# Dense expert values: sums kept in the eight PSUM banks and added once, tiles read by one 4 MB transfer in runs of 32 KB

## The reference, cut to what matters

```python
eidx = jnp.take_along_axis(cidx, sel, axis=-1).reshape(T, PEER_HEADS * PEER_TOPK)   # 128 experts per token
gate = jax.nn.softmax(sc, axis=-1).reshape(T, PEER_HEADS * PEER_TOPK).astype(c.dtype)
def expert_block(args):
    xb, idx, g = args
    act = jax.nn.gelu(jnp.einsum('td,tkd->tk', xb, u[idx]), approximate=False)
    return jnp.einsum('tk,tkd->td', g * act, v[idx])
```

## Time and profile before

| | |
|---|---|
| time, median of 3 runs | 3749.01 us (3737.89 to 3749.76) |
| the profiled execution's own time | 3740.18 us |
| its span | 3738.4 us |
| busy PE, DVE, ACT, POOL | 83%, 74%, 17%, 36% of the span |
| DMA | 1471.37 MB, mean 394 GB/s |
| build stage | about 2100 to 2376 us of the span |
| dense stage (L1239, L2212) | 2376 to 3379 us |
| embed beside the rows of SB, then the last block | 3379 to 3687, then to 3738 us |

### The profile page before, as it was taken

How to read it: one execution, slowest core, us unless ns; L and a number is a source line. 1 busy time by engine, 2 the same in 40 slices (tenths; PEclk the granted TensorE clock), 3 DMA queues, 4 the chain that set the end, 5 groups by cost and what they waited for, 6 DMA issues and landing times.

```text
span 3738.4 us, 26646 instructions
## 1 busy us (share of the span) xinstructions
PE 3101.5 (83%) x9234; PEld 1887.3 (50%) x9234; DVE 2756.7 (74%) x3846; ACT 636.9 (17%) x1610; POOL 1352.5 (36%) x908
## 2 busy tenths in 40 slices
PE   8998697999977359999988654799989899896955
PEld 4547343544456124455436643566666666563422
DVE  1005988677677869887866897978878899877785
ACT  2211110132011122122201366200000000002102
POOL 0001543325235434333333522423434342435552
PEclk9999798999988679999998856799999999998987
DMA  8889999999999999999999998999999999999997
GB/s 276 280 275 335 419 417 418 417 418 419 417 412 405 415 375 412 417 417 417 377 393 400 388 371 329 405 422 421 421 421 414 421 421 421 400 420 416 400 411 308
DMA packets 319143, 1471.37 MB, mean 394 GB/s; under 512 B 26080, under 2 KB 64416, under 8 KB 180768
## 3 DMA queue, kind: packets, MB, share of 16 engines
q0 software_dynamic: 129840, 944.83, 61.5%
q1 hardware_dynamic: 179136, 513.18, 36.1%
q10 hardware_dynamic: 10032, 11.66, 0.9%
HBM read 1443.88 MB, written 25.69 MB: 393 GB/s over the span
## 4 chain that ended last, share of the span: by engine, by line
DMA 39%; PE 22%; DVE 12%; issue 6%; POOL 6%; ACT 3%; SPq 0%; DVEq 0%; POOLq 0%; ACTq 0%
DMA ring<-in_peer_v,eidx 17%; PE psum L926 13%; DMA ring<-in_peer_u,eidx 11%; POOL ring L862 6%; DVE ring L2327 5%; DMA W<-in_w_peer_q 5%; DMA W<-in_w_out 2%; PE psum L904 2%; DVE arena L2339 2%; PE psum L1189 2%; DMA W<-in_w_ple_gate 1%; DMA a_scratch<-arena 1%; PE psum L1315 1%; ACT arena L1653 1%; DVE W L2195 1%
## 5 line engine op out<-in xcount | busy, mean ns | idle before, releaser
L2327 DVE CUSTOM_DVE_ANT_0 ring<-ring,cx 128x2048 f32<-128x2048 f32 x576 | 1312.5, 2285 | 235.1 <-DMA ring<-in_peer_u,eidx 232.3
L862 POOL DMA_INDIRECT ring<-in_peer_u,eidx x576 | 878.3, 1525 | 1676.4 <-DVE dots L2327 1255.1
L2339 DVE SCALAR_TENSOR_TENSOR arena<-ring,wts,arena 128x2048 f32<-128x2048 f32 x320 | 751.6, 2349 | 215.5 <-DMA ring<-in_peer_v,eidx 197.7
L926 PE MATMUL psum<-W,actT 128*128 128x512 f32 x1792 | 793.0, 601 | 19.2 <-DVE arena L2045 10.4
L862 POOL DMA_INDIRECT ring<-in_peer_v,eidx x320 | 469.1, 1466 | 617.9 <-DVE arena L2339 576.7
L926 PEld LDWEIGHTS psum<-W,actT 128*128 128x128 f32 x1792 | 342.0, 193 | 437.0 <-issue 420.3
L904 PE MATMUL psum<-W,actT 128*128 128x512 f32 x832 | 375.8, 608 | 42.4 <-issue 31.0
L1189 PE MATMUL psum<-actT,W 128*128 128x128 f32 (+2 forms) x1536 | 288.5, 353 | 83.1 <-DMA W<-in_w_peer_q 72.0
L1189 PEld LDWEIGHTS psum<-actT,W 128*128 128x128 f32 x1536 | 262.9, 208 | 107.8 <-DMA W<-in_w_peer_q 78.9
L904 PEld LDWEIGHTS psum<-W,actT 128*128 128x128 f32 x832 | 161.3, 196 | 243.4 <-issue 228.5
L1787 ACT ACTIVATE gel<-dots 128x8 f32<-128x8 f32 x72 | 15.1, 209 | 1572.8 <-DVE dots L2327 1572.7
(11 more groups left out here) (318 smaller groups left out, 2319.0 us busy)
## 6 DMA issues: line engine op xcount, KB each, us to landing
W<-in_w_in SPq DMA_DIRECT2D x168, 1024.0 KB
W<-in_peer_v SPq DMA_DIRECT2D x64, 1024.0 KB
arena<-in_peer_v SPq DMA_DIRECT2D x64, 1024.0 KB
W<-in_w_out SPq DMA_DIRECT2D x48, 1024.0 KB
W<-in_w_peer_q SPq DMA_DIRECT2D x48, 1024.0 KB
W<-in_w_ple_gate SPq DMA_DIRECT2D x39, 1024.0 KB
ring<-in_peer_u,eidx POOLq DMA_INDIRECT x576
a_scratch<-W SPq DMA_DIRECT2D x8, 1024.0 KB
```

Source lines behind the costliest of these rows:

```text
L862: pool.indirect_dma_start(ring[:, slot, :], None, a["peer_u" if what == "u" else "peer_v"][0], off(ix, 0)).then_inc(ring_in[slot], 16)
L926: ins = pe.matmul(bank(4 * s + j), lhs(at_k, j), w_pair(q)[:, k, s * CG:(s + 1) * CG], start=(at_k == 0), stop=(at_k == KT - 1))
L2327: dve.tensor_tensor_reduce(row, row, cx[:, :], 1.0, 0.0, ALU.mult, ALU.add, dots[:, n % DEEP, c:c + 1]).then_inc(u_used, 1)
L2339: dve.scalar_tensor_tensor(out=hslot(t), in0=ring[:, slot, :], scalar=wts[:, n % DEEP, c:c + 1], in1=hslot(t), op0=ALU.mult, op1=ALU.add). ...
```

## The change

Each tile is now one transfer of 4.19 MB in which partition p gets experts 4p to 4p + 3 of the tile, 32 KB in a row. So A's two indices change: within a tile's 512 experts the set is the number's lowest two bits, the partition the next seven. The results of all 32 tiles are summed in PSUM, in the eight banks, and DVE adds four times in all, at positions 529.6 to 532.6. The turn of `p` needs banks 6 and 7, so its wait for the adds moves ahead of it.

```diff
@@ row_landed
-                return tiles_in[k % 2], 16 * (VT * NVG // 2 + 1)
+                return tiles_in[k % 2], 16 * (NVG // 2 + 1)
@@ load_tiles
-            for x in range(VT):
-                e0 = (m * VT + x) * NKEY
-                sp.dma_start(v_tiles(m)[:, x, :], a["peer_v"][0, e0:e0 + NKEY, :]).then_inc(tiles_in[m % 2], 16)
+            e0 = m * VT * NKEY
+            sp.dma_start(v_tiles(m), a["peer_v"][0, e0:e0 + VT * NKEY, :].rearrange("(p x) d -> p x d", x=VT)).then_inc(tiles_in[m % 2], 16)
@@ pe_dense
-                pe.wait_ge(tiles_in[m % 2], 16 * VT * (m // 2 + 1))
+                pe.wait_ge(tiles_in[m % 2], 16 * (m // 2 + 1))
                 for i in range(4):
-                    at = 4 * m + i
-                    if at >= 3:
-                        pe.wait_ge(d_add, at - 2)
                     for half in range(2):
                         c0 = (i % 2 * 2 + half) * 512
                         for x in range(VT):
-                            ins = pe.matmul(bank(at % 3 * 2 + half), a_chunk(c)[:, i // 2 * P:(i // 2 + 1) * P, m * VT % CHUNK + x], v_tiles(m)[:, x, c0:c0 + 512],
-                                            start=(x == 0), stop=(x == VT - 1))
+                            ins = pe.matmul(bank(2 * i + half), a_chunk(c)[:, i // 2 * P:(i // 2 + 1) * P, m * VT % CHUNK + x], v_tiles(m)[:, x, c0:c0 + 512],
+                                            start=(m == 0 and x == 0), stop=(m == NVG - 1 and x == VT - 1))
@@ pe_embed
+            if 1 in ts:
+                pe.wait_ge(d_add, 4)
             pe.wait_ge(p_in, 16 if e == 0 else 16 * (NB + 1))
...
             pe.wait_ge(p_c, e + 1)
-            if 1 in ts:
-                pe.wait_ge(d_add, 4 * NVG)
@@ act_embed
-                act.wait_ge(d_add, 4 * NVG)
+                act.wait_ge(d_add, 4)
@@ dve_build
-                o.did(dve.tensor_scalar(parts["first_u"].bitcast(U32), eidx[:, eslot(t), :], 7, None, ALU.logical_shift_right))
-                o.did(dve.tensor_scalar(parts["second_u"].bitcast(U32), eidx[:, eslot(t), :], NKEY - 1, None, ALU.bitwise_and))
+                low, low_f = parts["indexT"][:, 0:P], parts["weightT"]
+                o.did(dve.tensor_scalar(parts["first_u"].bitcast(U32), eidx[:, eslot(t), :], 9, None, ALU.logical_shift_right))
+                o.did(dve.tensor_scalar(low.bitcast(U32), eidx[:, eslot(t), :], VT - 1, None, ALU.bitwise_and))
+                o.did(dve.tensor_scalar(parts["second_u"].bitcast(U32), eidx[:, eslot(t), :], 2, None, ALU.logical_shift_right))
                 o.wait()
+                o.did(dve.tensor_scalar(parts["second_u"].bitcast(U32), parts["second_u"].bitcast(U32), NKEY - 1, None, ALU.bitwise_and))
                 o.did(dve.tensor_copy(parts["first_f"], parts["first_u"].bitcast(U32)))
+                o.did(dve.tensor_copy(low_f, low.bitcast(U32)))
+                o.wait()
+                o.did(dve.scalar_tensor_tensor(out=parts["first_f"], in0=parts["first_f"], scalar=float(VT), in1=low_f, op0=ALU.mult, op1=ALU.add))
+                o.wait()
@@ dve_dense
-            for m in range(NVG):
-                for i in range(4):
-                    yield dense_at(m + 0.25 * (i + 1))
...
-                    dve.wait_ge(d_done, at + 1)
-                    if m:
-                        dve.wait_ge(d_add, at - 3)
-                    hc = hslot(DENSE[i // 2])[:, i % 2 * 1024:(i % 2 + 1) * 1024].rearrange("p (b c) -> p b c", b=2)
-                    dve.tensor_tensor(hc, psum[:, at % 3 * 2:at % 3 * 2 + 2, :], hc, ALU.add).then_inc(d_add, 1)
+            for i in range(4):
+                yield dense_at(NVG - 1 + 0.25 * (i + 1))
+                if i == 0:
+                    dve.wait_ge(added, DG * NB)
+                dve.wait_ge(d_done, 4 * (NVG - 1) + i + 1)
+                hc = hslot(DENSE[i // 2])[:, i % 2 * 1024:(i % 2 + 1) * 1024].rearrange("p (b c) -> p b c", b=2)
+                dve.tensor_tensor(hc, psum[:, 2 * i:2 * i + 2, :], hc, ALU.add).then_inc(d_add, 1)
```

More of the change, by code:

```diff
@@ L2199, in dve_dense @@
         def dve_dense(dve):
-            dve_waited = False
-            for m in range(NVG):
-                for i in range(4):
-                    yield dense_at(m + 0.25 * (i + 1))
-                    at = 4 * m + i
-                    if not dve_waited:
-                        dve.wait_ge(added, DG * NB)
-                        dve_waited = True
-                    dve.wait_ge(d_done, at + 1)
-                    if m:
-                        dve.wait_ge(d_add, at - 3)
-                    hc = hslot(DENSE[i // 2])[:, i % 2 * 1024:(i % 2 + 1) * 1024].rearrange("p (b c) -> p b c", b=2)
-                    dve.tensor_tensor(hc, psum[:, at % 3 * 2:at % 3 * 2 + 2, :], hc, ALU.add).then_inc(d_add, 1)
+            for i in range(4):
[5 more added lines that the diff above has]
+                dve.tensor_tensor(hc, psum[:, 2 * i:2 * i + 2, :], hc, ALU.add).then_inc(d_add, 1)
         def dve_embed(dve, e):
```

## The result

| | before | changed |
|---|---|---|
| median, all runs beside each other | 3742.27 us (3737.49 to 3749.76, 6 runs) | 3762.29 us (3753.65 to 3764.49, 6 runs) |
| ratio to before | | 1.0036, 95% interval 1.0019 to 1.0053 |
| the profiled execution | 3740.18 us, span 3738.4 | 3762.92 us, span 3761.1 |

A second series of the changed kernel gave 1.0047 (1.0031 to 1.0063). So it is slower by 0.4%: some 16 us by the mean of the two ratios, 1.0042, with intervals from 7 to 24 us (the two medians of the table are 20 us apart). 3744 and "no change" were forecast. Ratios are taken from fast executions alone, and the one profiled execution that was slow, of e8_paced_8k_runs, isn't read.

A forecast was written before the change was run, and what follows sets the result against it. After 2376 us the bytes to be moved up to the last gather, plus a fixed tail, set the time. 3740.18 + 10.5 - 11 + 2 + 0 = 3741.7, plus 2 toward the median: 3744 us, range 3722 to 3768.

The forecast's parts named there:

- The bound: Dense stage: after 2376 us the time is set by bytes to be moved up to the last gather, plus a fixed tail.
- The adds: Dense stage: 124 of 128 adds go, 151 us of DVE, and PE's 76.9 us of waits; by itself worth nothing at the end.
- The wait that takes the place of the removed one: SP's wait for SB's last pick ahead of tile 28: pick 23 us later, DMA runs empty while DVE limits, +10.5 us.
- The runs of 32 KB: Tile transfers: 4096 runs of 32 KB in place of 16384 of 8 KB save packet cost, -11 us.
- rival C: Long runs take four fifths of the DMA and starve gathers in the picks, +15 to +25 us: 3757 to 3767; chance 0.12.
- The start of the embed stage: Turn of p moves behind the last add, 2 to 3 us, covered by gathers: 0; without that cover 3.
- The longer split: Build stage: four more DVE instructions in each of two splits, +2 us; hidden: 0.
- The sum: Whole kernel: 3740.18 + 10.5 - 11 + 2 + 0 = 3741.7 us, plus 2 toward the median: 3744; chance 0.43.
- B: DVE, free of 151 us, keeps up with the gathers in the picks, so the DMA gets faster: 3725; chance 0.27.
- D: Runs are moved as pieces of 8 KB and only the wait shifts: 3753, up to 3755; chance 0.18.

The follow-up runs named there:

- e8_paced_8k_runs: e1_paced with each tile read by four transfers in runs of 8 KB, at the change's own places of the experts, first run: 1.0001.
- e14_held_to_27: Changed kernel with the hold (tile m waits until DVE has taken row 400 + 4m of u) for tiles 2 to 27 alone: 3756.24 us, 1.0023.
- e4_psum_only: Changed kernel with the old load_tiles (four transfers of 1.05 MB, runs of 8 KB) and the old split: 3764.93 us, 1.0054.
- e1_paced: Changed kernel, but SP holds each tile m until DVE has taken row 400 + 4m of u: 3750.70 us, 1.0009.
- e10_tile28_later: e1_paced with tile 28 held two rows more: 3749.86 us, 1.0002.
- e3_runs_only: Kernel before with the change's load_tiles (runs of 32 KB), tile counts and longer split, keeping the 128 adds: 3750.56 us, 1.0016.
- e2_inputs_last: Changed kernel with SP's wait for the last picks, and the inputs loaded behind it, moved behind the last tile: 3749.44 us, 1.0013.
- e13_wait_earlier: Changed kernel with SP's wait for the last pick, and the inputs behind it, ahead of tile 26 instead of tile 28: 3762.03 us, 1.0043.
- e9_last_tiles_held: e2_inputs_last with tiles 30 and 31 also held until row 400 + 4m of u: 3756.91 us, 1.0031.
- e15_held_from_28: Changed kernel with the hold at row 400 + 4m of u for tiles 28 to 31 alone: 3764.54 us, 1.0046.
- e6_split_only: Kernel before with four more DVE instructions in each of the two splits, their result unused: 3749.09 us, 0.9999.

## Why the prediction was wrong

**The bound** was read rightly: the DMA is busy nearly throughout behind 2425 us, and the times go with its idle time and packets, as the ledger shows over 17 executions of 15 kernels.

**The adds** went as put: 136 us of DVE and PE's waits gone, and no gain. The two series with the sums in PSUM, runs of 8 KB and the pace of before, 0.9988 and 0.9998, put the worth of both at 1 to 5 us, with intervals that reach to a loss of 4.

**The wait that takes the place of the removed one** came as worked out. Tile 27 was issued at 3104.57 (3092 forecast, its tiles began 12 us later than before, at 2417.91 for 2406.24), SP waited 108.9 us (110 forecast, though the forecast's own times, 3092 and 3211, make 119, so this agreement is partly luck), the pick came at 3214.1 (3211 forecast), PE stood still for 81.5 us (nearly 90). The term of +10.5 us was right in kind; the ledger has 9.5 us more idle there in the changed kernel and 7 in its second run, e14_held_to_27 puts it at 7.

**The runs of 32 KB** were the first step that failed: the term of -11. A packet of 8 KB took 313 ns and one of 32 KB 1219 (medians of the records), so four of the old ones are 33 ns dearer than one new, and 4096 of these over 16 engines are 8 us; the sum of all packets fell by 3.6 us from before to the changed kernel and by 9 from e4_psum_only. Against this stands what the prediction had only in rival C: the tiles took four fifths of the DMA while they landed, and a gather one fifth. In the picks, where C put 15 to 25 us, it costs little: from row 472 to the last pick 3.7 and 3.6 us are idle in e1_paced and e10_tile28_later, for 1.4 to 1.8 in the held kernels with runs of 8 KB. From the pick to the last add, SB's start in it, it is 6.6 and 5.8 for 1.9 to 2.3. All three idle columns sum to 17 or 18 us against 7 to 9 with runs of 8 KB. Net the term is about 0 in kernels at the old pace: e3_runs_only 1.0016, e1_paced 1.0009, e10_tile28_later 1.0002. Between e4_psum_only and the changed kernel, without the hold, it was -3 to -7.

The Trainium skill, "DMA: Bandwidth & Descriptors", section "Queues, rings and completion order", has an engine go round the queues packet by packet. The shares measured agree: equal packets would give half, 16 KB against 8 two thirds and 32 KB four fifths; the runs show 48%, 62% and 79 to 82%. The shares would come out alike if an engine took a transfer's eight packets at a time (128 packets over 16 engines), so how often it changes queue isn't shown.

**The start of the embed stage** was the second step that failed. It said "the gathers take the DMA in the meantime. 0; without that cover 3", and took as a sign of room that SP waited 58.6 us; but that wait ends at 3664 us, 280 us behind this place. The gathers can't: they wait for ring slots that DVE frees, and DVE itself waits for ACT there. What filled the DMA before were the last loads of SP. With all of `v` read earlier relative to DVE's rows, these were through: 6.2 us more idle (8.0 against 1.8). The prediction had counted that "the same bytes remain" but not when they come. e2_inputs_last and e14_held_to_27 show this hole without the first, e13_wait_earlier the first without this.

**The longer split** was put at +2 and is not to be told from 0 (0.9999).

**The sum** with the measured terms: 7 to 9 for the picks, about 6 for the embed stage, -4 to 0 for the packets, 0 for the split: 9 to 15 us, and 16 were measured. What is left, some 4 us, I can't place; it is less than the uncertainty of a ratio. The rivals: B (faster) is ruled out, D too, since a run was one packet, and C holds in the share that it gave the tiles, but not in its place and its size: its 3757 to 3767 holds the measured time for another reason, the pace of the tiles, so that agreement is luck. The forecast (its own range stands there once as 3736 to 3752 and once as 3734 to 3754) failed in saying "same" where the sum of two holes makes 0.4%.

## What to carry to other kernels

Where the DMA is the bound, a faster engine moves no byte; but it may draw the transfers that can run at any time ahead, and these are the cover for the places where the others must wait. So before freeing an engine, list the serial places of the rest (here the picks, a new block's first row, the norm of the embedding) and ask what is left in the queue at each; if the answer is nothing, hold the free transfers to the pace of the others (one wait: 20 to 25 us here with runs of 8 KB, 12 to 15 with 32 KB). A hole filled by moving such a transfer can open another where it was taken from (e9_last_tiles_held, e15_held_from_28).

## What the runs showed that I had not expected

- The time of code that didn't change varies more than the effects looked for. The first add of the dense stage waits for PE's first result, and this for the first chunk of A, which is read once the last write of A has landed, 8 to 22 us after its issue. In e3_runs_only and e6_split_only, whose profiled executions were among the longest of their kernels, DVE stood for 18.8 and 19.9 us there; in the kernel before it was 0.44 us. The row of the timeline of e6_split_only:

```profile
2413.83 1.23 DVE L2219 TENSOR_TENSOR arena<-psum,arena 128x1024 f32<-128x1024 f32 x1 [19.89 <-PE psum L1239]
```

  With one add at the end this wait can't occur. The build stage too began anywhere between 2120 and 2137 us, in the same code. A single profiled execution was off the median of its kernel by up to 14 us (e6_split_only, e9_last_tiles_held), and the 8.8 us between execution and median, which the prediction had to bridge, are within that.
